# Interleaving the top-16 searches of several lists, selecting over 560 candidate places instead of 800, and new rules in the planner that orders the stages

## What is computed

```
q = (xb @ wq).reshape(PEER_BLOCK, PEER_HEADS, 2, PEER_HALF)      # 8 heads, two halves
s = einsum('thcd,chkd->thck', q, keys)                           # 128 scores per half
sv, si = lax.top_k(s, 16)
cand = (sv[:, :, 0, :, None] + sv[:, :, 1, None, :]).reshape(.., 256)
cidx = (si[:, :, 0, :, None] * 128 + si[:, :, 1, None, :]).reshape(.., 256)
top, sel = lax.top_k(cand, 16)
eidx = take_along_axis(cidx, sel, axis=-1); gate = softmax(top)
act = gelu(einsum('td,thkd->thk', xb, u_tab[eidx]))
out = einsum('thk,thkd->td', gate * act, v_tab[eidx])
```

## Time and profile before

| | us |
|---|---|
| median of 3 runs (1940.42 to 1944.46) | 1942.24 |
| the profiled execution, its own time | 1939.56 |
| span of its profile | 1937.8 |
| DVE busy | 1095.3 (57%) |
| PE busy | 1034.4 (53%) |
| POOL busy | 1156.0 (60%) |
| ACT busy | 173.9 (9%) |

### The profile page before, as it was taken

The page is one execution under the profiler, slowest core; times in us unless marked ns, Lnnn a source line. Parts: engine busy times, 40 slices in busy tenths (PEclk is TensorE's granted clock), DMA queues, the critical chain, the costliest instruction groups (busy, mean ns, idle before and its releaser), DMA issues.

```text
span 1937.8 us, 18049 instructions
## 1 busy us (share of the span) xinstructions
PE 1034.4 (53%) x6274; PEld 477.3 (25%) x6274; DVE 1095.3 (57%) x2851; ACT 173.9 (9%) x297; POOL 1156.0 (60%) x1062
## 2 busy tenths in 40 slices
PE   7867230574754654717655766465854640035556
PEld 3433120332311232304111333332311120021113
DVE  1266898867920467888800486968950179960001
ACT  2222010000100011100000022101100010000001
POOL 0033556254677766676677767456576787777770
PEclk9888665687878876758778978777876675568888
DMA  7577767697999999999999999899799999999993
GB/s 294 190 297 283 260 223 283 181 380 294 385 409 409 409 413 412 372 377 353 410 409 409 405 407 408 275 359 399 256 401 410 409 404 409 409 409 409 409 409 144
DMA packets 173192, 687.24 MB, mean 355 GB/s; under 512 B 19856, under 2 KB 21520, under 8 KB 158366
## 3 DMA queue, kind: packets, MB, share of 16 engines
q0 software_dynamic: 152064, 553.72, 73.1%
q1 hardware_dynamic: 21038, 132.37, 18.0%
HBM read 679.88 MB, written 6.59 MB: 354 GB/s over the span
## 4 chain that ended last, share of the span: by engine, by line
DMA 32%; POOL 24%; PE 17%; DVE 15%; issue 11%; ACT 1%; SPq 0%; DVEq 0%; ACTq 0%; POOLq 0%
POOL rows L1182 24%; DMA rows<-in_v,index_tb 10%; DMA rows<-in_u,index_A 7%; PE bank L728 7%; DMA rows<-in_v,index_ta 7%; PE acc L1010 6%; DMA rows<-in_u,index_B 4%; DVE rows L1747 4%; DMA wring<-in_w 1%; DVE scratch L1570 1%; DMA rows<-in_v,index_S 1%; DVE scratch L1644 1%; PE bank L725 1%; DVE scratch L1694 1%; DVE scratch L1693 1%
## 5 line engine op out<-in xcount | busy, mean ns | idle before, releaser
L1182 POOL DMA_INDIRECT rows<-in_u,index_A x256 | 325.3, 1271 | 365.6 <-DVE index_A L1722 178.4
L1010 PE MATMUL acc<-rows,wz 128*32 128x512 f32 x2048 | 341.4, 798 | 289.2 <-DMA rows<-in_v,index_tb 142.8
L728 PE MATMUL bank<-wring,turned 128*128 128x512 f32 x832 | 410.3, 645 | 69.9 <-DVE decayed L1454 33.0
L1182 POOL DMA_INDIRECT rows<-in_u,index_B x256 | 299.8, 1171 | 108.8 <-issue 71.0
L1747 DVE SCALAR_TENSOR_TENSOR rows<-rows,xn_a 128x1024 f32<-128x1024 f32 x256 | 304.7, 1224 | 79.9 <-DMA rows<-in_u,index_A 76.6
L1182 POOL DMA_INDIRECT rows<-in_v,index_ta x256 | 252.6, 987 | 145.0 <-PE acc L1010 78.2
L1747 DVE SCALAR_TENSOR_TENSOR rows<-rows,xn_b 128x1024 f32<-128x1024 f32 x256 | 306.9, 1226 | 56.7 <-DMA rows<-in_u,index_B 51.1
L1182 POOL DMA_INDIRECT rows<-in_v,index_tb x256 | 242.3, 946 | 107.7 <-issue 61.9
L728 PEld LDWEIGHTS bank<-wring,turned 128*128 128x128 f32 x832 | 165.6, 208 | 272.5 <-issue 245.9
L1010 PEld LDWEIGHTS acc<-rows,wz 128*32 128x32 f32 x2048 | 74.0, 127 | 532.9 <-issue 510.7
L1780 DVE TENSOR_TENSOR x_b<-x_b,acc 128x1024 f32<-128x1024 f32 x2 | 2.4, 1222 | 260.6 <-PE acc L1010 260.6
(11 more groups left out here) (293 smaller groups left out, 997.5 us busy)
## 6 DMA issues: line engine op xcount, KB each, us to landing
wring<-in_w SPq DMA_DIRECT2D x108, 1024.0 KB, 8.1
scratch<-in_c_s SPq DMA_DIRECT2D x2, 2064.0 KB, 11.1
out_c_s<-scratch SPq DMA_DIRECT2D x2, 2064.0 KB, 9.9
rows<-in_u,index_A POOLq DMA_INDIRECT x256, 11.4
rows<-in_v,index_ta POOLq DMA_INDIRECT x256, 7.7
rows<-in_u,index_B POOLq DMA_INDIRECT x256, 9.2
rows<-in_v,index_tb POOLq DMA_INDIRECT x256, 7.9
keys<-in_keys SPq DMA_DIRECT2D x2, 1024.0 KB, 9.8
```

The source lines that it names most:

```text
L728: ins = pe.matmul(ps[:, :], turned["A"][:, 4 * h + c, :], w[:, c, :], start=first, stop=end, skip_group_check=True)
L1010: ins = pe.matmul(acc[i * QUAD:(i + 1) * QUAD, c, :], wz[:, i, g * QUAD:(g + 1) * QUAD], row, start=first, stop=end, skip_group_check=True)
L1182: pool.indirect_dma_start(out=rows[:, n % RING, :], out_offset=None, in_=a[table], in_offset=bass.IndirectOffsetOnAxis(ap=which[:, at:at + ...
```

## The change

`top16` takes several lists and goes through them step by step: the first instruction for all lists, then the second for all, each waiting only for its own list's. `rank` and `best` take ranges (4 lists, or 2 in the first quarter of pass 0; 2 heads). `pairs` writes the candidate sums in another order, so that the 20 that can be among the best 8 (`EARLY`) come first, and `best` looks up the first 8 places among 20 candidates and the other 8 among 50: 8 x 20 + 8 x 50 = 560 elements a head instead of 800, for both heads in one instruction of each kind. In later passes `pairs` takes 4 heads at a time. `woven` has three new rules, and three costs of the planner differ. The scratch tile is laid out anew and `by_head` has a tile of its own.

```diff
+EARLY = sum(TOPK // 2 // (a + 1) for a in range(TOPK // 2))
+HOT = TOPK // 2 * (EARLY + CANDS)
...
+        for h0, h1 in ((0, 1), (1, 2)) if (p, j) == (0, 0) else ((2 * j, 2 * j + 2),):
+            add("rank", big, 2 * h0, 2 * h1)
+            if p == 0:
+                add("pairs", big, h0, h1)
+                add("best", big, h0, h1)
+                add("soften", big, h0, h1)
+                add("choose", big, h0, h1)
+        if p and j % 2:
+            add("pairs", big, 2 * j - 2, 2 * j + 2)
+            add("best", big, 2 * j - 2, 2 * j)
+            add("best", big, 2 * j, 2 * j + 2)
...
+MARGIN = 8.0
...
         if not for_real:
-            return idle, start if start is not None else now
+            held = sum(us for engine, us in self.steps(e) if engine in engines)
+            return idle, start if start is not None else now, held + idle
...
+        elif half_done and groups[0][0] == "dots" and KIND[groups[0][1]] == "S":
+            take = "stage"
+        elif groups[0][0] in ("gelu", "weights", "add"):
+            take = "group" if of_group[1] <= of_stage[1] + 0.5 else "stage"
+        elif blocked == "slot" and of_group[0] <= 0.3 and of_group[1] + of_stage[2] > clocks.dma - MARGIN:
+            take = "group"
         elif stages[0][0] in RANKING and blocked != "index":
...
+            def top16(lists):
+
+                half = TOPK // 2
+                highest = [marked(dve.max(values[:, 0:half], src)) for values, _, src in lists]
+                located = []
+                for (values, idx, src), n in zip(lists, highest):
+                    dve.wait_ge(vector_step, n)
+                    located.append(marked(dve.max_index(idx[:, 0:half], values[:, 0:half], src)))
...
+                dve.wait_ge(vector_step, last_located)
...
+                for hot, width, k in ((early, EARLY, slice(0, half)), (late, CANDS, slice(half, TOPK))):
+                    equal = marked(dve.tensor_tensor(hot, place[:, :, :, 0:width].to_broadcast([m, n, half, width]),
+                                                     sought[:, :, k, :].to_broadcast([m, n, half, width]), ALU.is_equal))
...
-                step(dve.tensor_tensor(hot, down(const("place", m), TOPK), across(best_f[0:m, h, :], CANDS), ALU.is_equal))
-                step(dve.tensor_tensor(hot, hot, down(codes[0:m, h, :], TOPK), ALU.mult))
-                step(dve.tensor_reduce(chosen[0:m, h, :], hot, AX.X, ALU.add))
```

More of the change, by code:

```diff
@@ L175, in stage_front @@
             out.remove(entry)
-            out.insert(out.index(("rank", big, 0)), entry)
+            out.insert(out.index(("rank", big, 0, 2)), entry)
     return out
@@ L341, in steps @@
             out = (("PE", 1.2), ("ACT", 1.6)) + out
-        if stage == "pairs" and not small:
-            out = (("DVE", 1.3 + 0.7 * (e[3] - e[2])),)
+        if stage == "rank":
+            out = (("DVE", 0.4 + 1.2 * (e[3] - e[2])),)
+        if stage == "best":
+            out = (("DVE", 1.0 + 2.5 * (e[3] - e[2])),)
         return out
@@ L393, in woven @@
 def woven(groups, stages, clocks, out):
-    groups, stages, waited = list(groups), list(stages), 0
+    groups, stages, waited, half_done = list(groups), list(stages), 0, set()
     def emit(e):
@@ L399, in emit @@
         out.append(e)
+        if e[0] in ("project", "mix", "query", "gate"):
+            half_done.symmetric_difference_update([(e[0], e[2], e[4])])
     while groups or stages:
```

106 lines of the change are left out of this document (60 added, 46 removed).

## The result

The changed kernel takes 1909.76 us (median of 4 runs, 1907.35 to 1919.32) beside 1941.33 us (4 runs, 1937.94 to 1944.46) of the kernel before on the same chip: a ratio of 0.9845, with a 95% interval of 0.9823 to 0.9867. It is faster, as forecast, but by 31.6 us and not by 68: 1909.8 lies just outside the range of 1840 to 1906.

What follows compares the result with a forecast made beforehand. Transfers at 410 GB/s need 1676 of 1937.8 us; of 262 lost, 180 can be won, with DVE setting the end in tile 0's `choose` stretches. Terms -49 + 9 - 28 = -68 off the 1942.24 median give 1874 us, range 1840 to 1906.

Steps and rivals of the forecast that it cites:

- Up to `gelu` of tile 0: Tile 0's start: shorter ranking and sample work moved behind `gelu` bring `gelu` from 457 to 383 us, -74.
- From `gelu` to `add` of tile 0: Tile 0's `vals` stretch: moved weight halves and store add 33.4 us, 9 lost; 215 us instead of 190.2.
- pass 1: From `add` of tile 0 to `add` of tile 1: 23 us lost against 12.1 and some 2, so +9.
- up to the last `dots` of tile 1 transfers bound it, as before: In pass 1, transfers still set the pace until the last `dots` of tile 1.
- 5 elsewhere: Pass 1 outside the chain behind the last `dots` of tile 1: 5 us of transfer lost.
- 8 us for each long run of `dots` from a full ring: Unbroken `dots` rows slow gathers to 1.99 + 0.30 us, draining a full ring at half supply; about 8 us lost.
- The chain behind it: Behind tile 1's last `dots`: 55 us of `mix`, `query`, lists and other stages against 36 of transfers; 18 lost.
- To `gelu` of tile 3: From 1223.6 us, ring full: 52 rows, 5 us of stages and 5 for half-rate start, 70 instead of 119.9, -50.
- To `add` of tile 3: From `gelu` of tile 3: 176.4 us of transfer + 33.4 + 9 = 219 instead of 197.1, +22.
- 2, chained or not: Chaining makes no difference: a quarter's ranking costs 17.3 instead of 14.9 us; 1882 us, chance 0.08.
- Rival 1: The `vals` stretches keep their losses and the chain costs 10 more, swallowing half the gain; 1904 us, chance 0.17.
- or if the gather at 1.99 us becomes the common one: Closing sign in the profile after that would show the forecast wrong: POOL's slow gathers become the usual ones.

Runs made afterwards that it cites:

- Run 4: The changed kernel with one more wait after each prompt row of `dots`, so rows follow at 1.265 us; 1887.23 us, ratio 0.975 to the kernel before.
- run 13: The changed kernel, unpaced, with `turn_index` of tiles 1, 3 and 4 and the stages behind it only after group 26 of `vals`; 1895.49 us, ratio 0.9754.
- its control: The changed kernel itself, run again in the same group on the same chip; 1909.29 us, ratio 0.985 to the kernel before.
- run 5: The changed kernel and order, but each list's five search instructions chained one behind the other; 2053.33 us on a slower chip, ratio 1.0146 to the kernel before.

## Why the prediction was wrong

- **Up to `gelu` of tile 0** (-74) it was right: -73.7, and each `choose` within 5 us. The operations cost less than forecast: four lists 4.8 us instead of 5.5, a pair of heads 5.9 (1.68 for the searches, 4.2 for cast and look-up) instead of 6.75, because a list of searches loses 0.6 us of its 1.83 by not waiting and not 0.53. Yet the `choose` come 1 to 5 us later than forecast, and what holds them was not tried.
- **From `gelu` to `add` of tile 0** (+25) it was right: +27.0.
- **The step that failed is pass 1**, in "up to the last `dots` of tile 1 transfers bound it, as before" and "5 elsewhere". The text had the rate at which a gather is locked out, 1.99 + 0.30 us, and named 8 us for each long run of `dots` from a full ring. For pass 1 it took over the behaviour of before, where `mix` and `query` stand between these rows, and did not ask whether the run of 60 rows, which the changed order puts between `pool` and `mix` (place 3), starts from a full ring and with no other transfer beside it. It does, and loses 19 us instead of 5: 7.1 while the rows stand back to back, close to the 8, and 12 more behind that, which the 8 do not cover. Run 4 cuts the run to 76.0 us and its loss to 3.5 by the pace alone. The chain behind it, which I took for the risk, was charged 18 and cost 11.7; it takes 52.8 us there and 52.1 in run 4, where it loses 17.8 because the run ahead of it has left the ring fuller. Behind the first `vals` 8.2 us go where nothing was charged; PE's 8.0 us at `turn_index` lie there, but run 13, which removes them, has no shorter pass 1, so that part is open.
- **To `gelu` of tile 3** (-50) the size was off: from the first of the last 52 rows to `gelu` it took 76.4 us where I had 70, 71.9 with the pace. The mechanism is the same (68.2 us at 330 GB/s are 13.3 lost, where I had 5), but since run 4 leaves the stretch as a whole at 226.1 us, it explains 4.5 of the 8 us at most.
- **To `add` of tile 3** (+22) it was +29.8. The missing term is PE's wait at `turn_index`, 12.94 us. In the prediction the order of the ranking in the `vals` stretch was costed only by DVE's total ("does not bound them"), not by when its last piece is done. Run 13 brings the stretch to 218.3, 6.5 us less than its control.
- **Rivals.** 2, chained or not, is false (run 5). Rival 1, `vals` stretches that swallow half, gave the nearest time (1904), and its mechanism holds 10 of the missing 38 us. The missing case was a rival in which the unbroken runs cost more. My last sentence, "or if the gather at 1.99 us becomes the common one", points at the mechanism, but had no price and no chance, and as it stands it did not come true: 81 gathers take over 1.7 us, against 108 before. Where they fall matters, not how many there are.
- That the time stands only 4 us outside the range is in part luck: the first two steps were right, and in pass 1 the chain, charged 6 us too much, hid some of what the run of rows cost.
- Two small slips stand in the sums and change nothing: three times 1.41 us is 4.2 and not 4.3, and 3.70 + 1.08 is 4.8 and not 4.7.
- The parts of this change don't add up: 0.4% won, 2.2% lost, 1.6% won together. The prediction's sum worked for both together only because it was done on the final order.

## What to carry to other kernels

When two engines meet at a shared resource, compare the times at which each is ready for its turn, not their loads: a producer that is back 1.11 us behind the end of a row comes just too late, with the next row but one begun, when rows follow at a pitch of 1.145 us, and in time at 1.265, and slowing the consumer by a tenth made the kernel 1% faster on the chip of the result. If a change makes a run of one instruction unbroken, look for another place in the same trace where that run exists, see from which state it starts (full or empty ring) and what else moves beside it, and charge what it loses there. Where the engine that waits for an index is in order, put the instruction that fetches it as late as its first reader allows, and cost a ranking by when it ends, not by its sum.
